# One more step between the scores, exponentials and values of four attention stages in a two-block transformer kernel

## The reference

```python
for i in range(2):                      # first block
    h = x @ w_in[i]
    a = dsa_attention(q, k, v, qi, ki, wi)      # 8 heads of 64, keys chosen by an index score
    b = spatial_gating(gelu(u), gelu(vs), ...)
    x = layer_norm(ALPHA * x + concat(a, b) @ w_o[i])
    x = layer_norm(ALPHA * x + ffn(x) + ple(x))
# second block, layer 0 (even)
y = concat(dense_causal_attention(q, k, v),     # 8 heads of 96, from low-rank latents
           dilated_mixture(qd, kd, vd)) @ w_out # 4 heads, one softmax over 3 groups
# second block, layer 1 (odd)
o_c = diff_causal_attention(q, k, v, lam)       # 4 heads: softmax(1) - lam * softmax(2)
o_c = rms_norm(o_c, diff_subln) * (1 - lam_init)
y = concat(o_c, moba_attention(qm, km, vm)) @ w_out   # 8 heads of 64
# both: x = x + g1 * y; x = x + g2 * squared_relu_mlp(modulate(rms_norm(x)))
```

## Time and profile before

| | |
|---|---|
| median of three runs | 1347.8 us (1346.65 to 1350.24) |
| the profiled execution | 1350.45 us |
| its span, first to last instruction | 1348.6 us |
| PE busy | 1291.3 us (96%) |
| DVE busy | 922.1 us (68%) |
| ACT busy | 653.7 us (48%) |
| POOL busy | 114.0 us (8%) |
| mean DMA rate | 200 GB/s |

### The profile page before, as it was taken

The page is one execution under the profiler, slowest core; times in us unless marked ns, Lnnn a source line. Parts: engine busy times, 40 slices in busy tenths (PEclk is TensorE's granted clock), DMA queues, the critical chain, the costliest instruction groups (busy, mean ns, idle before and its releaser), DMA issues.

```text
span 1348.6 us, 15871 instructions
## 1 busy us (share of the span) xinstructions
PE 1291.3 (96%) x6342; PEld 1065.4 (79%) x6342; DVE 922.1 (68%) x1237; ACT 653.7 (48%) x884; POOL 114.0 (8%) x146
## 2 busy tenths in 40 slices
PE   8999999998999999999999899999999968999998
PEld 6878888887877888887788777888878756888886
DVE  6968777766787677775778747766667874744444
ACT  6645444442563544444564536545446553654542
POOL 2001000001001000000334100000004400000000
PEclk9999999999999999999999989999999988999999
DMA  9626677864634678884353205867755411444450
GB/s 377 236 75 227 240 304 302 319 247 156 213 115 147 207 295 307 310 307 162 112 189 125 79 32 189 323 268 272 289 218 187 157 63 34 183 171 183 180 187 32
DMA packets 41113, 270.35 MB, mean 200 GB/s; under 512 B 4656, under 2 KB 4672, under 8 KB 12880
## 3 DMA queue, kind: packets, MB, share of 16 engines
q1 hardware_dynamic: 38288, 259.83, 52.2%
q0 software_dynamic: 2464, 8.98, 1.8%
q10 hardware_dynamic: 288, 0.52, 0.1%
HBM read 268.27 MB, written 1.05 MB: 200 GB/s over the span
## 4 chain that ended last, share of the span: by engine, by line
PE 79%; DVE 12%; ACT 5%; issue 2%; POOL 1%; DMA 0%; ACTq 0%; DVEq 0%; POOLq 0%
PE ps L1573 47%; PE ps L1563 24%; PE ps L1587 4%; DVE WB L1888 3%; PE ps L1675 2%; ACT E L1688 1%; PE ps L1650 1%; ACT WB L1688 1%; DVE st L2104 1%; POOL st L1490 1%; ACT H L1688 1%; DVE st L2174 1%; DVE SCR L2006 1%; ACT XTH L1688 1%; DVE H L2258 0%
## 5 line engine op out<-in xcount | busy, mean ns | idle before, releaser
L1888 DVE TENSOR_TENSOR WB<-RAW,WB 128x2048 fp32r<-128x2048 f32 (+3 forms) x211 | 452.8, 2151 | 235.9 <-ACT WB L1688 235.6
L1688 ACT ACTIVATE WB<-RAW 128x2048 fp32r<-128x2048 f32 (+3 forms) x211 | 379.9, 1802 | 218.5 <-PE ps L1573 214.8
L1563 PE MATMUL ps<-WB,XTH 128*128 128x512 f32 (+3 forms) x1176 | 314.0, 388 | 9.3 <-ACT XTH L1688 4.4
L1573 PE MATMUL ps<-WB,XTH 128*128 128x512 f32 (+3 forms) x1176 | 306.6, 382 | 9.7 <-DVE WB L1888 9.6
L1573 PE MATMUL ps<-WB,XTL 128*128 128x512 f32 (+3 forms) x1176 | 304.4, 380 | 0.9 <-DVE XTL L1961 0.5
L1573 PEld LDWEIGHTS ps<-WB,XTH 128*128 128x128 f32 x1176 | 218.1, 189 | 53.8 <-DVE WB L1888 15.2
L1563 PEld LDWEIGHTS ps<-WB,XTH 128*128 128x128 f32 x1176 | 213.6, 190 | 49.5 <-ACT XTH L1688 7.8
L1573 PEld LDWEIGHTS ps<-WB,XTL 128*128 128x128 f32 x1176 | 219.0, 189 | 40.3 <-DVE XTL L1995 0.8
L1563 PE MATMUL ps<-WB,HTH 128*128 128x512 f32 (+1 forms) x452 | 126.9, 396 | 0.6 <-ACT HTH L1688 0.5
L1573 PE MATMUL ps<-WB,HTH 128*128 128x512 f32 (+1 forms) x452 | 126.5, 395 | 0.0
L1573 PE MATMUL ps<-WB,HTL 128*128 128x512 f32 (+1 forms) x452 | 126.4, 394 | 0.0
(11 more groups left out here) (179 smaller groups left out, 961.3 us busy)
## 6 DMA issues: line engine op xcount, KB each, us to landing
RAW<-W SPq DMA_DIRECT2D x220, 1024.0 KB, 4.9
RAW<-W SPq DMA_DIRECT2D x22, 768.0 KB, 4.3
VEC<-vecd POOLq DMA_DIRECT2D x10, 512.0 KB, 6.5
RAW<-W SPq DMA_DIRECT2D x8, 512.0 KB, 3.7
RAW<-W SPq DMA_DIRECT2D x4, 576.0 KB, 3.7
RAW<-W SPq DMA_DIRECT2D x2, 648.0 KB, 3.9
T<-sgwd POOLq DMA_DIRECT2D x2, 512.0 KB, 8.5
X<-xd SPq DMA_DIRECT2D x1, 1024.0 KB, 18.3
```

The lines of the kernel that those rows point to most:

```text
L1563: eng.matmul(banks[b][:, 0:cw], x2[j][0], hi[:, j, c0:c0 + cw], start=first and j == 0, stop=False)
L1573: op = eng.matmul(banks[b][:, 0:cw], x2[j][0 if low_w else 1], (lo if low_w else hi)[:, j, c0:c0 + cw], start=False, stop=last and end and ...
L1688: return eng.activation(dst, src, f, **k)
L1888: eng.tensor_tensor(WB[:, it["raw"], 0:w], RAW[:, it["raw"], 0:w], WB[:, it["high"], 0:w].bitcast(F32), ALU.subtract).then_inc(*up("wl", n))
```

## The change

All units are one step deeper. Step k now emits the turns of unit k-2, `differ` and `joint` of unit k-1, and the values of unit k-3, and there are n + 3 steps instead of n + 2. A score unit may overwrite its buffer of `E` once the transposes of the unit two before have read it (before: once their copies were made); as these transposes now come in the same step behind the scores, `turns` hands that event on to the later unit.

Around it: `pads`, `flush` and `quiet` go; held subtractions are emitted in each `advance` and at the end of every step below n - 2. The `steps` lists are new. In the odd attention `diff_norm` of tile 0 and 1 moves from the filler to steps 5 and 8, and `linear_k` goes by tile instead of by piece. In both attentions of the second block the transposes of the first four heads for the output product are no longer made ahead of it by `out_start` but by `ready`, just before their product. Some transposes of tile 1's heads move ahead of the first scores, and `turn_groups(0)` moves from step 6 to step 5.

```diff
@@ advance
-            if not cur["quiet"]:
-                lows()
+            lows()
@@ linear_k(..., by_tile=True) -> linear_k(...)
-            for it, t in ([(it, t) for t in range(2) for it in its] if by_tile else
-                          [(it, t) for it in its for t in range(2)]):
+            for it, t in [(it, t) for t in range(2) for it in its]:
@@ attention
-                u["e_free"] = e_free[i]
+                u["e_free"] = list(e_free[i])
...
-            def turns(u, pad):
+            def turns(u, after):
                 i = u["i"]
                 u["t"] = turn([E[:, i, c:c + 128] for c in u["blocks"]], [u["x"]] + p_free[i],
-                              lambda a, c: PET[...], 128, pad)
-                e_free[i] = [u["t"][-1]]
+                              lambda a, c: PET[...])
+                e_free[i] = [("tp", u["t"][-1][1])]
+                if after:
+                    after["e_free"][:] = e_free[i]
...
-            for k in range(n + 2):
-                cur["quiet"] = k in quiet
+            for k in range(n + 3):
...
-                if 1 <= k <= n:
-                    turns(units[k - 1], pads[k - 1] if k <= len(pads) else 0)
-                if k < n and units[k]["diff"]:
-                    ends(units[k])
+                if 2 <= k < n + 2:
+                    turns(units[k - 2], units[k] if k < n else None)
+                if 1 <= k <= n and units[k - 1]["diff"]:
+                    ends(units[k - 1])
...
-                if k in flush:
+                if k < n - 2:
                     lows(old)
-                if k >= 2:
-                    values(units[k - 2])
+                if k >= 3:
+                    values(units[k - 3])
@@ first block
-            attention(units, fill, first=1, pads=(0, 2, 2))
+            attention(units, fill, (1, 1, 1, 1, 1, 1, 0, 0, 0), first=1)
@@ even
-                turn_heads(0)
+                turn_heads(0, 0, 1)
-                ahead = {6: [lambda: turn_groups(0)]}
-                between = {0: [lambda: turn_heads(1)], 6: [lambda: turn_groups(1)]}
-                steps = (4, 3, 2, 2, 2, 1, 1, 0, 2, 1, 1, 1, 1, 1, 1, 1)
-                pads, flush, quiet = (), (0, 1, 2, 3, 6, 7, 8, 9, 10, 11), (4,)
+                ahead = {0: [lambda: turn_heads(1, 0)]}
+                between = {0: [lambda: turn_heads(1, 1)], 5: [lambda: turn_groups(0)], 6: [lambda: turn_groups(1)]}
+                steps = (4, 3, 2, 2, 2, 0, 0, 1, 1, 1, 1, 1, 1, 1, 0, 0, 0)
@@ odd
-                ahead = {}
-                between = {0: [lambda: turn_qk(tw, 1, (0, 0), (1, 4)), ch[3, 0][0], ch[3, 1][0]],
+                ahead = {0: [lambda: turn_qk(tw, 1, (0, 0))]}
+                between = {0: [lambda: turn_qk(tw, 1, (1, 4)), ch[3, 0][0], ch[3, 1][0]],
...
+                           5: [lambda: normed.pop(0)()], 8: [lambda: normed.pop(0)()]}
-                steps = (1, 1, 1, 1, 1, 1, 2, 1, 1, 1, 1, 1)
-                pads, flush, quiet = (0, 0, 0, 2), (0, 1, 5, 6, 7), (3,)
+                steps = (1, 1, 1, 1, 0, 0, 1, 0, 0, 1, 0, 0, 0)
@@ output product, even and odd
             def ready(a, t):
-                if a:
-                    while "out" not in keys_[2 + t]:
-                        yield
-                    xo_w[t].extend(to_XT(MIX, n_out, ..., t, pad=2 if t else 0, base=4, both=t == 0))
-
-            def out_start():
-                for t in range(2):
+                if a == 0:
                     while "out" not in keys_[t]:
                         yield
-                    if normed:
-                        normed.pop(0)()
                     xo_w[t].extend(to_XT(MIX, 4, [keys_[t]["out"]], t))
+                    return
+                if t == 0 and i == 0:
+                    gain(0, 0)
+                while "out" not in keys_[2 + t]:
                     yield
-                    if t == 0 and i == 0:
-                        gain(0, 0)
-                        yield
-                yield from linear_k(nm_out, xo_w, gated_put(i, 0, 0, xg), ready, by_tile=i == 0)
-
-            fill = chain(fill, out_start())
+                xo_w[t].extend(to_XT(MIX, n_out, ..., t, pad=2 if t else 0, base=4, both=t == 0))
+
+            fill = chain(fill, linear_k(nm_out, xo_w, gated_put(i, 0, 0, xg), ready))
```

More of the change, by code:

```diff
@@ L296, in program @@
         cur = {"chunk": 0, "item": 0, "load": 0, "ahead": 0, "pairs": 3, "id": 0, "col": 0, "turn": 0, "buf": 0,
-               "lag": False, "quiet": False}
+               "lag": False}
         bufs = [(n, []) for n in range(NBUF)]
@@ L411, in linear, with linear_k @@
             yield
-        def linear_k(name, lhs, evac, ready, turned=False, by_tile=True):
+        def linear_k(name, lhs, evac, ready, turned=False):
             its = chunk_items(name)
@@ L591, in program, with attention @@
         p_free = [[], []]
-        def attention(units, filler=None, steps=1, pads=(), first=0, ahead={}, between={}, flush=None, quiet=()):
+        def attention(units, filler=None, steps=1, first=0, ahead={}, between={}):
             n = len(units)
-            flush = range(n - 2) if flush is None else flush
             def scores(u, pad):
@@ L637, in ends @@
                     do("joint", u)
-            def turns(u, pad):
+            def turns(u, after):
                 i = u["i"]
                 u["t"] = turn([E[:, i, c:c + 128] for c in u["blocks"]], [u["x"]] + p_free[i],
-                              lambda a, c: PET[:, i, a * 128:(a + c) * 128].rearrange("p (n q) -> p n q", n=c), 128, pad)
-                e_free[i] = [u["t"][-1]]
+                              lambda a, c: PET[:, i, a * 128:(a + c) * 128].rearrange("p (n q) -> p n q", n=c))
+                e_free[i] = [("tp", u["t"][-1][1])]
+                if after:
+                    after["e_free"][:] = e_free[i]
             def values(u):
@@ L675, in attention @@
                     ends(units[k - 1])
-                if k in flush:
+                if k < n - 2:
                     lows(old)
-                if k >= 2:
-                    values(units[k - 2])
-            cur["lag"] = cur["quiet"] = False
+                if k >= 3:
+                    values(units[k - 3])
+            cur["lag"] = False
         def normalised(ok, dst, sums, nh, dv):
@@ L1166, in program, with turn_heads @@
                 tw = [[], []]
-                def turn_heads(t):
-                    for n, (x_, base) in enumerate(((MQ, 0), (MK, 8))):
+                def turn_heads(t, *ns):
+                    for n in ns:
+                        x_, base = ((MQ, 0), (MK, 8))[n]
                         tw[t] += turn_T([x_[:, t, h * 96:h * 96 + 96] for h in range(8)], mr[n, t] + t_pe, base, t, 96,
@@ L1289, in ready @@
             def ready(a, t):
-                if a:
-                    while "out" not in keys_[2 + t]:
-                        yield
-                    xo_w[t].extend(to_XT(MIX, n_out, [keys_[2 + t]["out"]], t, pad=2 if t else 0, base=4, both=t == 0))
-            def out_start():
-                for t in range(2):
+                if a == 0:
                     while "out" not in keys_[t]:
                         yield
-                    if normed:
-                        normed.pop(0)()
                     xo_w[t].extend(to_XT(MIX, 4, [keys_[t]["out"]], t))
+                    return
+                if t == 0 and i == 0:
+                    gain(0, 0)
+                while "out" not in keys_[2 + t]:
                     yield
-                    if t == 0 and i == 0:
-                        gain(0, 0)
-                        yield
-                yield from linear_k(nm_out, xo_w, gated_put(i, 0, 0, xg), ready, by_tile=i == 0)
-            fill = chain(fill, out_start())
+                xo_w[t].extend(to_XT(MIX, n_out, [keys_[2 + t]["out"]], t, pad=2 if t else 0, base=4, both=t == 0))
+            fill = chain(fill, linear_k(nm_out, xo_w, gated_put(i, 0, 0, xg), ready))
             for t in range(2):
@@ L1342, in program @@
                                           outs=outs, blocks=[c * 128 for c in range(2 * per * (t + 1))]))
-            attention(units, fill, steps, pads, 0, ahead, between, flush, quiet)
+            attention(units, fill, steps, 0, ahead, between)
             t_pe = [keys_[3]["op"]]
```

2 lines of the change are left out of this document (1 added, 1 removed).

## The result

The kernel after took 1358.1 us (median of 4 runs, 1355.9 to 1358.4) beside 1347.3 us for the kernel before: ratio of the means 1.0072, 95% interval 1.0053 to 1.0091. It is slower by 0.7% (9.7 us), where the prediction had 1341 us and 15% for any slowdown.

A forecast was written before the change was run, and what follows sets the result against it. TensorE, busy 96% of the span, was taken as the bound, with time to win in its idle and half-clock stretches. Odd 6.5 + even 4.0 - first block 4.0 = 6.5 us won, giving 1341, own range 1337 to 1346.

The forecast's parts named there:

- First block, -4.0: First block's two attentions: a new wait and later tail outweigh the pads removed, 4.0 us lost for both.
- four pads go, 1.2 us: First block, each attention: dropping four throw-away matmuls that fill gaps wins 1.2 us.
- small share for the clock after the new 2.1 us wait: First block: half clock behind TensorE's new wait takes the loss for both layers from 3.4 to 4.0 us.
- Odd, +6.5: Odd attention, second block: shorter waits for the normalised heads, less losses further on, win 6.5 us.
- Another wait of 2.4 us: Odd attention: the product waits 2.4 us for ScalarE's half of its transposes, queued behind the exponentials of M5 and M6.
- Minus 1.1 us: Odd attention, step 8: tile 1's multiplies ahead of M5's normalising delay the second product's transposes, 1.1 us lost.
- costs nothing: Odd attention: a 2.15 us VectorE subtraction ends just before the sum needs VectorE, so no time is lost.
- +0.5 and +0.6: Odd attention: 0.5 us less half clock up to the first product, perhaps 0.6 us at the product at 1140.43.
- Even, +4.0: Even attention, second block: a wait removed and less half clock in the slow stretch, less new waits, win 4.0 us.
- (a): All stages: more waits go than counted and no stretch falls to half clock; 15 us won, 1333, chance 0.22.
- (b): Grouped units: PSUM banks block the added depth; odd wins 5, even 0, first block loses 4; about 1347, chance 0.16.
- (c): Even attention's steps 8 to 12 and the first block's drains fall to half clock; 1354, chance 0.14.

The follow-up runs named there:

- pads_in_wait: Kernel after, plus nine throw-away matmuls ahead of the gated values' transposes in each first-block attention; 1.0036 against the kernel before.
- first_block_only: Kernel before, with only the first block's attention (both layers) one step deeper; 1.0065 against the kernel before.
- pads_back: Kernel after, with the four removed pads put back in each first-block attention, ahead of the turns of units 0 and 1; 1.0027 against the kernel before.
- weights_behind: Kernel after, with ScalarE's copy of the next weight issued behind the filler product's own operand copy; 1.0003 against the kernel before.
- weights_low: weights_behind, with the odd attention's VectorE subtraction of the next weight held from step 7 until step 9; 0.9992 against the kernel before.
- best_pads: best, with twelve throw-away matmuls ahead of odd tile 0's normalised-row transposes and nine ahead of the product behind them; 0.9917 against the kernel before.
- best: First block of the kernel before joined to the second block of weights_low; 0.9941 against the kernel before.
- best_split: best, with the odd attention's first filler product one step behind the transposes of its left operand; 0.9901 against the kernel before.
- odd_only: Kernel before, with only the odd attention (layer 1, second block) one step deeper; 1.0015 against the kernel before.
- even_only: Kernel before, with only the even attention (layer 0, second block) one step deeper; 1.0002 against the kernel before.

## Why the prediction was wrong

The sum had 6.5 us won; 9.7 were lost. One of its signs of being wrong came: the odd stage won less than 4 us. And the first block's stages grew by 5.1 and 3.7 us instead of 1.5.

**First block, -4.0: the sign was right, the size not.** The steps that failed are "four pads go, 1.2 us" and the "small share for the clock after the new 2.1 us wait", 0.6 us. The pads did not fill gaps only; with them the clock stayed up, and PE came later to a wait that ends when DVE is done anyway. The predicted wait came (2.1 us; 2.18 and 2.08 measured), and so did what does not hang on the clock: in pads_in_wait, where the clock is 1.00, the stages are 2.0 and 2.1 us longer than before, and 1.7 were predicted. But half clock behind the wait took 3.3 and 1.8 us where 0.6 stood for both layers. first_block_only puts the whole term at 1.0065, 8.8 us; in pads_back and pads_in_wait 6.1 and 4.9 us of run time come back with the clock kept. In the one profile of first_block_only the even attention behind it was 3.3 us longer too (99.5 against 96.2) and the odd one 1.3 us shorter; whether that is the first block's doing is not shown.

**Odd, +6.5: it was -2 (0.3 to 3.9 lost).** This is the largest miss. The first wait was right (2.5; 2.86 measured), so was the tail (1.6 and 0.5; 1.66 and 0.34). Up to the first product the stage won 5.4 us where 7.5 were predicted (51.1 us from its start to 1115.62, against 58.5 before, less the 2.0 us of work still to do), and lost 5.7 behind it. Three terms were wrong. "Another wait of 2.4 us" was 3.57, because the list of ACT's queue left out the weight copy that the product's start puts ahead of its own copy. "Minus 1.1 us" for the second product was 2.92, because the subtraction in front of the multiplies was given no cost ("costs nothing" was worked out for the first tile only). And half clock, credited with +0.5 and +0.6: the second credit came (the product at 1143.66 takes 1.23 us, its counterpart at 1140.43 took 1.93), but the rows at 1115.62 to 1120 and 1132.3 to 1137 lose 2.3 and 2.5 us, and in sum the slow rows of the stage lose 7.9 us where they lost 7.2. weights_behind and weights_low show the first two as causes of their waits; the third only as far as best_pads goes, where the product's half clock vanished with the pads.

**Even, +4.0: nothing over the runs (1.1 us won to 1.8 lost), 1.7 us in the profile.** The slow drain went, as forecast: the rows of the stage that ran at half clock exceed their full-clock durations by 7.0 us in sum before and by 1.7 after. But PE's waits of 0.5 us and more grew from 8.7 to 11.6 us; the one predicted at 2.6 us was 3.62, for such a weight copy, and the one at the turned groups 1.55 where 1.0 was predicted. With the copy out of the way the stage reads 91.5 us. That the profile shows a gain and the runs none fits the kernel before: its profiled execution lies 2.65 us above its median.

**The rivals.** (a) was wrong: more waits came, not fewer. (b) had nothing won in the even attention, as the runs show, but not by its mechanism: steps 9 to 12 have no wait above 0.88 us, as the prediction said; and it would have left the odd gain standing, which did not come. (c) named the right mechanism, the clock, and nearly the right time (1354), but in the wrong place: the even stage's steps 8 to 12 ran at full clock (0.98 over the stage), and half clock came mostly behind waits of 2 us and more, in the first block above all. That the time came near 1354 is luck. Of the rule of the Trainium skill quoted there the traces bear out that the clock swings between its levels, in the first block too (0.92 and 0.96), but there behind one wait of 2.2 us; the short idles of the even stage's drain (0.88 us and less) did not bring it about. Against that, the end of the odd stage ran at half clock in weights_low, best and its follow-ups with no wait above 1.14 us shortly ahead of it. The chance of 0.14 for (c) was too low for a kernel whose two attention stages already showed 0.90 and 0.93.

## What to carry to other kernels

A wait can have two prices: its own length, and what PE does at half clock behind it (1.8 to 3.5 us behind one of 2.1 or 2.2 us in the first block). Its length alone does not tell: in the kernel before PE ran on at full clock behind a wait of 2.11 us, and at half clock behind the shorter ones of 1.83 and 1.64. So ask of each new wait what runs behind it and what that would lose at half clock, and of each pad that is taken out whether it stands in front of a wait. When a queue is written out by hand, write out what the helper functions emit on their own (here the next weight's copy and subtraction), since a product that follows its own transposes at once waits for all that stands before its own copy; and when one is moved, look who stands behind it in its new place, as in weights_low. And deepen one stage at a time: here even and odd attention with the queue mended, one product a step later (best_split) and the first block left alone give 0.990, and the whole as it was 1.007.

## What the hardware showed that was not expected

- Nine matmuls of no use (2.1 us) in front of eight transposes in each layer of the first block brought the run from 1.0072 to 1.0036: 4.9 us (1.5 to 8.3).
- The same even attention, instruction for instruction, took 96.2 us (before), 96.3 (odd_only) and 99.5 us (first_block_only); its three longest waits were the same within 0.01 us (2.11, 1.83 or 1.84, 1.64) and its clock 0.93 or 0.90. With one profile of each it is open whether the first block, 290 us before it, or chance made the difference.
- Where an execution falls to half clock is partly chance: the same products at 20 to 24 us ran partly at half clock in the profile of the kernel after and at full clock in that of first_block_only, behind waits of 1.15 and 1.13 us.
- even_only took 1346.9 to 1349.6 us in 12 runs, the kernel before 1344.7 to 1352.1 in 28 beside it. The deeper even stage has a higher clock in its profiles (0.96 to 1.00, 0.90 or 0.93 with the old loop), but that it narrows the spread is not shown: weights_low and best have it too and took 1343.8 to 1350.2 and 1336.0 to 1343.7 us.
